# Decode step, one core: masks of group A's products copied to contiguous rows by GpSimd, and queries and keys of group B stored with 80 rows instead of 73

## What is computed

```python
def fox_prompt(qb, b_kv, lf):                       # group B, prompt
    c = jnp.cumsum(lf, axis=1)
    ...
    logits = jnp.einsum('bqgrd,bkgd->bgrqk', q, kb) * HEAD_DIM ** -0.5
    logits = logits + (c_q - c_k)
    logits = jnp.where(kpos[None, :] <= qpos[:, None], logits, -jnp.inf)
    p = jax.nn.softmax(logits, axis=-1)
    return jnp.einsum('bgrqk,bkgd->bqgrd', p, vb)

def dsa_sample(qa, a_kv, qi, ki, wi, pos, cache_a_kv, cache_idx_k, page_table, l, topk):   # group A, samples
    sc = jnp.concatenate([indexer_scores(qi, wi, ki_past), indexer_scores(qi, wi, ki)], -1)
    idx, valid = select_topk(sc, (kpos[None, :] <= pos[:, None])[None], topk)
    ...
    return sparse_attend(qa, kv_sel, valid)
```

## Time and profile before

| | |
|---|---|
| median of 3 runs | 4775.23 us (4770.79 to 4775.99) |
| the profiled execution's own time | 4774.78 us |
| its span, first to last instruction | 4773.0 us |
| mean granted TensorE clock | 0.909 |
| PE busy | 4119.1 us, 86% |
| PEld busy | 3288.7 us, 69% |
| DVE busy | 2801.5 us, 59% |
| ACT busy | 1716.9 us, 36% |
| POOL busy | 606.8 us, 13% |
| products that open group A's sums, L2032 | 64, mean 1108 ns |
| queries of B in the prompt, L721 | 16 loads of 292 KB |

### The profile page before, as it was taken

How to read it: one execution, slowest core, us unless ns; L and a number is a source line. 1 busy time by engine, 2 the same in 40 slices (tenths; PEclk the granted TensorE clock), 3 DMA queues, 4 the chain that set the end, 5 groups by cost and what they waited for, 6 DMA issues and landing times. The chain is left out here.

```text
span 4773.0 us, 63369 instructions
## 1 busy us (share of the span) xinstructions
PE 4119.1 (86%) x24094; PEld 3288.7 (69%) x24094; DVE 2801.5 (59%) x5139; ACT 1716.9 (36%) x2589; POOL 606.8 (13%) x695
## 2 busy tenths in 40 slices
PE   7999377688877888877788799888999999999997
PEld 5878244455555555555546544778999999999997
DVE  4333289989999999998335433553344353343533
ACT  3333234444444444553442223213233233232331
POOL 0222300000000000000267730000000000000000
PEclk9999667878889889888898888999999999999998
DMA  3333301000000000000367751434444544445442
GB/s 135 125 111 118 108 28 32 21 21 16 17 16 12 12 17 17 10 8 5 121 216 217 240 195 36 161 120 135 130 118 124 137 121 128 124 128 139 120 127 63
DMA packets 460725, 444.91 MB, mean 93 GB/s; under 512 B 26728, under 2 KB 405299, under 8 KB 460484
## 3 DMA queue, kind: packets, MB, share of 16 engines
q1 hardware_dynamic: 403396, 256.46, 18.9%
q0 software_dynamic: 57104, 185.42, 11.5%
HBM read 371.71 MB, written 69.95 MB: 93 GB/s over the span
## 5 line engine op out<-in xcount | busy, mean ns | idle before, releaser
L507 DVE TENSOR_SCALAR_CACHE_REDUCE at_relu<-at_scores,at_cand 128x272 f32<-128x272 f32 (+14 forms) x480 | 685.2, 1427 | 9.4
L1524 PE MATMUL ff_ps<-ff_h_high,ff_w_high 128*128 128x412 f32 x1760 | 619.7, 352 | 25.0 <-DVE ff_w_low L1618 25.0
L1525 PE MATMUL ff_ps<-ff_h_low,ff_w_high 128*128 128x412 f32 x1760 | 615.8, 350 | 0.0
L1526 PE MATMUL ff_ps<-ff_h_high,ff_w_low 128*128 128x412 f32 x1760 | 613.5, 349 | 0.0
L1618 DVE TENSOR_TENSOR ff_w_low<-ff_w_raw,ff_w_high 128x2048 fp32r<-128x2048 f32 (+1 forms) x150 | 375.7, 2504 | 188.8 <-ACT ff_w_high L1573 188.8
L961 ACT ACTIVATE at_probs<-at_probs,at_nmax 128x144 f32<-128x144 f32 (+15 forms) x256 | 311.0, 1215 | 461.7 <-DVE at_nmax L1043 461.2
L1573 ACT ACTIVATE ff_w_high<-ff_w_raw 128x2048 fp32r<-128x2048 f32 (+1 forms) x150 | 311.5, 2076 | 360.1 <-PE ff_ps L1526 357.9
L974 ACT ACTIVATE at_pT_sb<-tr 128x512 f32<-128x512 f32 x544 | 304.8, 593 | 326.6 <-PE tr L847 326.1
L827 PE MATMUL S<-at_kbT,at_queries_b 73*128 73x512 f32 (+16 forms) x768 | 310.6, 546 | 116.4 <-DVE at_nmax L1043 62.0
L847 PE MATMUL tr<-ident,at_probs 128*128 128x128 f32 x2176 | 345.6, 304 | 10.4 <-ACT at_pT_sb L974 5.5
L1524 PEld LDWEIGHTS ff_ps<-ff_h_high,ff_w_high 128*128 128x128 f32 x1760 | 331.4, 188 | 27.7 <-issue 25.8
(11 more groups left out here) (326 smaller groups left out, 7559.9 us busy)
## 6 DMA issues: line engine op xcount, KB each, us to landing
ff_w_raw<-in_w_gate SPq DMA_DIRECT2D x110, 512.0 KB, 4.0
ff_w_raw<-in_w_up SPq DMA_DIRECT2D x110, 512.0 KB, 5.2
ff_w_raw<-in_w_down SPq DMA_DIRECT2D x80, 704.0 KB, 6.2
out_PN<-pn POOLq DMA_DIRECT2D x17, 1000.0 KB, 6.2
at_q_raw<-dram_QTA SPq DMA_DIRECT2D x124, 128.0 KB, 2.8
x_in<-in_x_rows SPq DMA_DIRECT2D x17, 512.0 KB, 3.9
dram_HN<-x_in POOLq DMA_DIRECT2D x17, 512.0 KB, 7.7
dram_QTA<-qaiT POOLq DMA_DIRECT2D x17, 512.0 KB, 5.4
```

What stands on the lines that cost most here:

```text
L507: return v.tensor_scalar(out, x, cand.bitcast(F32), 0.0, ALU.is_ge, ALU.add, accum_out=cnt)
L1524: pe.matmul(out, w_high[p][:, w], high, start=first, stop=False)
L1525: pe.matmul(out, w_high[p][:, w], low, start=False, stop=False)
L1526: return pe.matmul(out, w_low[p][:, w], high, start=False, stop=last)
```

## The change

Two edits. The first makes `AUG` 80: the last place of a query row moves from 72 to 79, places 72 to 78 are 0 in the queries, and the keys have 1 in places 72 to 79. Every buffer, product and transfer of group B in the prompt has 80 rows for 73. The second lets GpSimd copy each step's mask, 8 partitions of 512 values, into one of four contiguous buffers (in `lf` and `bias`, which group B no longer needs by then), and lets the product read it from there.

```diff
-AUG = HD + HEADS + 1
+AUG = HD + HEADS + HEADS
...
-            pool.memset(k_aug[:, :, AUG - 1:AUG], 1.0)
+            pool.memset(k_aug[:, :, HD + HEADS:AUG], 1.0)
...
+        masks = [of[0:NB].rearrange(how)[:, k * 512:(k + 1) * 512]
+                 for of, how in ((lf, "p a b n -> p (a b n)"), (bias, "p r b n -> p (r b n)")) for k in range(2)]
...
+            def make_mask(n):
+
+                c, hf, k = (n - 16) // 2, n % 2, n - 16
+                if k == 0:
+                    pool.wait_ge(moved, 64)
+                    pool.wait_ge(lf_step, 4 * 16)
+                    pool.wait_ge(opened, 16)
+                if k >= 4:
+                    pool.wait_ge(opened, 16 + k - 3)
+                two = scores[:, 2 * c * SPLIT_W:(2 * c + 2) * SPLIT_W].rearrange("b (c n) -> b c n", n=SPLIT_W)[:, :, 0:SPLIT_W - 1]
+                keys = two.rearrange("b c (p r) -> b r c p", r=RUN_A)[:, 4 * hf:4 * hf + 4]
+                pool.wait_ge(laid_out, 5 + k)
+                pool.tensor_copy(masks[k % 4].rearrange("b (r c p) -> b r c p", r=4, c=2), keys).then_inc(laid_out, 1)
+
             for c in range(8):
                 at = c % 4
+
+                for n in (16, 17, 18, 19) if c == 3 else (2 * c + 10, 2 * c + 11) if c > 4 else ():
+                    make_mask(n)
                 pool.wait_ge(pv_done, 13 + c if c < 4 else 16 + 2 * (c - 3))
                 for b in range(NB):
                     gather(kv[:, at, b, :], CACHE_A, runs_a[:, b, c:c + 1], a_here[at])
+            for n in range(26, STEPS):
+                make_mask(n)
...
             def open_a(n):
-                c, hf = (n - 16) // 2, n % 2
                 pe.wait_ge(moved, 64)
                 pe.wait_ge(exp_done, n - 1)
...
-                two = scores[:, 2 * c * SPLIT_W:(2 * c + 2) * SPLIT_W].rearrange("b (c n) -> b c n", n=SPLIT_W)[:, :, 0:SPLIT_W - 1]
-                keys = two.rearrange("b c (p r) -> b r c p", r=RUN_A)[:, 4 * hf:4 * hf + 4]
+                pe.wait_ge(laid_out, 5 + n - 16 + 1)
                 for u in range(2):
-                    pe.matmul(S[:, 2 * (n % 2) + u, :], expand[:, u, :], keys, start=True, stop=False)
+                    ins = pe.matmul(S[:, 2 * (n % 2) + u, :], expand[:, u, :], masks[(n - 16) % 4], start=True, stop=False)
+                ins.then_inc(opened, 1)
```

More of the change, by code:

```diff
@@ L1769, in decode @@
         runs_done = sem("runs_done")
-        zeroed = sem("zeroed")
+        laid_out = sem("laid_out")
         staged = sem("staged")
@@ L1791, in decode @@
         bias_done = sem("bias_done")
-        bias_used = sem("bias_used")
+        opened = sem("opened")
         qk = sem("qk")
@@ L1886, in _ @@
         def _(pool):
-            pool.memset(flat[:, 1024:2048 + P], 0.0).then_inc(zeroed, 1)
-            pool.memset(w_sel[:], 0.0).then_inc(zeroed, 1)
-            pool.memset(lf_later[:], 0.0).then_inc(zeroed, 1)
+            pool.memset(flat[:, 1024:2048 + P], 0.0).then_inc(laid_out, 1)
+            pool.memset(w_sel[:], 0.0).then_inc(laid_out, 1)
+            pool.memset(lf_later[:], 0.0).then_inc(laid_out, 1)
             def gather(to, rows, at, signal):
@@ L1898, in _ @@
                 if c == 0:
-                    pool.memset(bias[:], 0.0).then_inc(zeroed, 1)
-                    pool.memset(suffix[:, RUN_B - 1, :], 0.0).then_inc(zeroed, 1)
+                    pool.memset(bias[:], 0.0).then_inc(laid_out, 1)
+                    pool.memset(suffix[:, RUN_B - 1, :], 0.0).then_inc(laid_out, 1)
             for s in range(16):
@@ L2014, in open_b @@
                         ins = pe.matmul(S[:, 2 * (n % 2) + u, r * P:(r + 1) * P], heads, ident[:], start=(r == 0), stop=False)
-                ins.then_inc(bias_used, 1)
+                ins.then_inc(opened, 1)
             def open_a(n):
-                c, hf = (n - 16) // 2, n % 2
                 pe.wait_ge(moved, 64)
@@ L2111, in _ @@
             act.wait_ge(tr_full, 1)
-            act.wait_ge(zeroed, 3)
+            act.wait_ge(laid_out, 3)
             def heads(at, rows):
@@ L2195, in _ @@
                 v.tensor_scalar(runs[:, cols], pages[:, cols], float(units), pmod[:, k:k + 1], ALU.mult, ALU.add).then_inc(runs_done, 1)
-            v.wait_ge(zeroed, 3)
+            v.wait_ge(laid_out, 3)
             of_i = new[:, QI:QI + 512].rearrange("p (h d) -> p h d", d=HD)
@@ L2258, in make_bias @@
                 if n == 0:
-                    v.wait_ge(zeroed, 5)
+                    v.wait_ge(laid_out, 5)
                 else:
-                    v.wait_ge(bias_used, n)
+                    v.wait_ge(opened, n)
                 v.wait_ge(lf_step, 4 * (n + 1))
```

## The result

The changed kernel takes **4715.73 us** (median of 4 runs, 4713.50 to 4721.16), the kernel before, run beside it, 4775.04. The ratio is 0.9879, with a 95% interval of 0.9862 to 0.9896: 59 us or 1.2% faster, against 45 forecast. The profiled executions have spans of 4773.0 and 4711.6, 61.4 us apart.

| stretch | before | after | difference | forecast |
|---|---|---|---|---|
| start to the first issue of the prompt's attention | 525.10 | 513.01 | -12.1 | -5.3 |
| from there to GpSimd's first query | 22.43 | 6.83 | -15.6 | -15.2 |
| to the end of the search of tile 1 (the scan, L538) | 75.81 | 73.58 | -2.2 | -2.5 |
| tiles 2 to 15, to the decode's first issue | 1720.15 | 1714.51 | -5.6 | 0 |
| decode, to the point where PE is ready for the first mask of group A | 402.31 | 403.18 | +0.9 | 0 |

A forecast was written before the change was run, and what follows sets the result against it. DVE was taken to bound the prompt's attention, PE the decode's group A. Terms -15.2 - 2.5 - 5.3 - 33.1 + 10.4 + 1.0 = -44.7 us against 4774.78 gave 4730.1, forecast as 4730.5, range 4716 to 4748.

The forecast's parts named there:

- Stage's start: Start of the prompt's attention: quicker small loads let q_raw land earlier, moving GpSimd's chain by -15.2 us.
- Tile 1: Prompt's attention, tile 1: group B's queries land 9.5 us earlier, DVE loses 7 more beside GpSimd's subtractions: -2.5 us.
- The projection's end: Last tile's wait for the keys' store -2.3 us, last store before the barrier -3.0, other fifteen tiles 0: -5.3.
- The masks on PE: Decode, group A: four contiguous mask passes take 1.8 us for 3.84, 2.07 less a step, 16 times: -33.1 us.
- The first mask: Decode step 16: the mask copy stands behind chunk 2's eight gathers, so PE stands for 10.4 us.
- The clock behind the stall: After the first mask's wait PE is at half clock for a few us, costing +1.0 us.
- Steps of 12.0: Decode, group A: each step shortens from 14.0 to 12.0 us.
- rival 1: Group A's clock stays up with contiguous products, gaining up to 0.5 us in 15 steps: 4723 us; chance 0.15.
- Rival 2: GpSimd's mask copies take 4 us each, lengthening the first stall and four later ones: 4742 us; chance 0.09.
- rival 3: Transfers of 80 rows go like 73, leaving only the decode's -21.7 us: 4753.5 us; chance 0.06.
- rival 4: Eight rows, not the stride, slow the mask product; PE gains nothing and still stands: 4763.6 us; chance 0.03.
- rival 5: Slower: GpSimd bounds group A's step with copies above 10 us; 4782 us at 12 us a copy; chance 0.02.

The follow-up runs named there:

- the strides: The kernel before, its group A mask products reading 512 values straight from the scores at steps of 1 to 8 or 16 values, without GpSimd copies: 4758.41 us.

## Why the prediction was right, and where it was off

The direction, both mechanisms and the stall were right; 14.8 us more were saved than I forecast, and the time lies 0.3 us under the range's lower end of 4716.0. Point by point, by the terms of the sum:

- **Stage's start, -15.2:** measured -15.6, and the chain went as written (first product after 4.2 us, forecast 4 to 5).
- **Tile 1, -2.5:** measured -2.2, and both of its parts were a little smaller than forecast: the first product of group B comes 8.1 us earlier against GpSimd's first query (forecast 9.5), and the loss to GpSimd is 5.9 us more (forecast 7; L525 takes 14.0 us where it took 8.2). That the two errors nearly cancel is luck. The loss was also wrong in its reason: I counted four subtractions, but the copies hold DVE too, 0.97 and 0.98 us in two of them.
- **The projection's end, -5.3: mis-sized.** Ten profiled executions with 75 or 80 rows begin the attention at 513.0 to 515.9 (mean 514.7), four with 73 or 79 at 524.4 to 526.0 (525.1): -10.4. The last store and the barrier behind it gave 5.1 in this pair and not 3.0 (from the last L254 12.84 us before, 7.69 after; 5.6 in the means of the four and the ten), since GpSimd's issue fell as well, by 1.7 us, and the store landed in under 4. The wait at the last tile gave 2.9 against 2.3. The term that I had put at nothing, the fifteen tiles ahead, gave 2.9 in this pair and 1.9 in the mean, and my reading there was wrong: in single tiles PE does wait for the store, by way of DVE's copy. In the kernel before, DVE (first row) and then PE (second):

```profile
299.73 0.42 DVE L482 COPY kT_out<-pQ 128x256 f32<-128x256 f32 x1 [5.22 <-DMA dram_KTD<-kT_out]
300.59 0.66 PE L301 MATMUL pQ<-ident,q_aug 128*73 128x128 f32 x4 [1.91 <-DVEq L485]
```

PE's usual wait there is 0.6 us. It was longer in four tiles of this execution (0.72, 0.86, 0.99 and 1.91 us, 2.1 more in all), in one to three tiles of the other three with 73 or 79 rows (up to 2.03 us), and in none of four that I read with 75 or 80. That the changed kernel shows -12.1 has 1.3 us in it that were there at the first of these stores (97.3 against 96.0), ahead of any store of 73 or 80 rows.

- **Tiles 2 to 15, 0:** right; the -5.6 of this pair of executions is spread.
- **The masks on PE, -33.1:** 16 times 1.93 are -30.9. The contiguous group holds PE for 1.91 us, and not for the 1.8 that I had put together from 0.43 a pass and the change of operands.
- **The first mask, +10.4:** 11.4. The copy is 1.1 us and not 0.9, and the gathers began 0.55 us after PE was ready and not 0.53 before.
- **The clock behind the stall, +1.0: mis-sized,** 3.0.
- **Later masks, 0:** four waits of 0.16 to 0.19. The slack of 0.9 was worked out from steps of 12.0 us; they are 11.1, so it was gone, and the run with two copies of each mask shows it.
- **Steps of 12.0: too long.** This is the step that failed by kind: I left the clock at 0.88 and gave its rise a chance of 0.15 (rival 1). Group A's difference is -25.6; the terms above give -30.9 + 11.4 + 3.0 + 0.7 = -15.8, which leaves -9.8 for the clock. Rival 1 had 0.5 us in 15 steps, 7.5. This is the largest term that the forecast lacked. It shows little in the sum, as 5.9 us stand against it (2.2 of the passes, 1.0 and 2.0 of the stall and the clock behind it, 0.7 of the later waits). Between the two profiled executions 16.7 us more were saved than forecast: 3.9 in group A, 6.8 at the projection's end and 5.6 in tiles 2 to 15, the last of which is luck, and 0.4 elsewhere.

Rival 2 (copies of 4 us) falls with 1.1 us; rival 3 with the result itself and the run with 80 rows alone; rival 4 with the strides; rival 5 with the length of the copy. Two sums of the prediction are off without touching the forecast: its own ends add up to 4746 at the top and not 4742, and by its 10 us of gathers and two copies in 24 us GpSimd would fill the two steps from copies of 7 us on, not 10 (rival 5). Not settled: which steps of group A fall to the lower clock. The same kernel has steps of 11.1 and 12.1 us with the same work, and no run here took that apart.

## What to carry to other kernels

Give a DMA a row count with a large divisor up to sixteen; 73 to 75 rows is enough, and a slow transfer that keeps the old count keeps its price. Look in the trace which transfers are slow: here SP's loads and GpSimd's store of keys were, GpSimd's other transfers of 73 rows were not. Lay the fp32 operand that PE streams (its moving one) out so that at least two of the values read share 16 bytes, and if another engine makes the layout, put its work ahead of its long queue items, not behind them: the stall that the first order made cost 11.4 us and about 3 more through the clock. Slack that is worked out from the old step length has to be worked out again with the new one.

## What the runs showed of the hardware that I had not expected

- A step of 3 values costs half of what a step of 4 does (2.95 us against 3.84, from 1.98), and a step of 2 almost nothing (2.06).
- GpSimd's copy with one input holds DVE's one-value instruction as long as a subtraction does: until it ends.
- GpSimd's own loads of 73 rows were not slow. Its two of 511 KB landed in 10.2 us in the kernel before, against 11.8 for 560 KB with 80 rows, where SP's 292 KB took 21.8 (566.08 to 587.88). Nor was its store of queries of 73 rows: 292 KB landed in a median 6.0 us, issued in 0.54, against 5.8 for 320 KB with 80 rows. Its store of keys of 73 rows was slow, 8.8 us for 73 KB against 5.2 for 80 KB, and slow to issue (2.35 us, 2.49 with 79 rows, 0.71 with 75, 0.63 with 80). What sets the keys' store apart is not shown.
- Reading the masks with a step of 8 values cost 1.93 us a step of the decode by itself, at a granted clock of 1.00, and 0.87 more through the lower clock of the work behind it.
